# mLSTM layer in fp32: q, k, v and o projections as seven quarter products through DRAM, output projection beside the chunks

## The reference

```python
u = rmsnorm(h, mix_norm_g)
q, k, v, o_pre, if_pre = split(u @ w_in)       # 512, 512, 1024, 1024, 16 columns; k times 64 ** -0.5
# gates -> log_i, log_f; then over chunks, with a carried state (c_st, n_st, m_st):
scores = (qc @ kc.T) * exp(log_d - m_t)
num = w_inter * (qc @ c_st) + scores @ vc ;  den = w_inter * (qc @ n_st) + sum(scores)
hh = num / max(|den|, exp(-m_t)) ;  c_st, n_st updated from w_k and vc
h = h + (rms(hh) * norm_g * sigmoid(o_pre)) @ w_out
u = rmsnorm(h, ffn_norm_g)
h = h + (silu(u @ w_gate) * (u @ w_up)) @ w_down
```

## Time and profile before

| | us |
|---|---|
| median of 3 runs | 2203.44 (2202.58 to 2205.53) |
| the profiled execution | 2202.67 |
| its span, first to last instruction | 2200.7 |
| TensorE (PE) busy | 2170.1 |
| VectorE (DVE) busy | 1306.2 |
| ScalarE (ACT) busy | 883.4 |
| GpSimd (POOL) busy | 187.3 |

### The profile page before, as it was taken

The page is one execution under the profiler, slowest core; times in us unless marked ns, Lnnn a source line. Parts: engine busy times, 40 slices in busy tenths (PEclk is TensorE's granted clock), DMA queues, the critical chain, the costliest instruction groups (busy, mean ns, idle before and its releaser), DMA issues.

```text
span 2200.7 us, 29564 instructions
## 1 busy us (share of the span) xinstructions
PE 2170.1 (99%) x10600; PEld 1804.0 (82%) x10616; DVE 1306.2 (59%) x1990; ACT 883.4 (40%) x1520; POOL 187.3 (9%) x263
## 2 busy tenths in 40 slices
PE   7999999999999999999999999999999999999999
PEld 6888888878888888888888888888788888887887
DVE  6325666286656575678652366644865756656764
ACT  5224455253333333345422335552533333333443
POOL 2000110020101010100010011000210100101000
PEclk9999999999999999999999999999999999999999
DMA  4112124213232324863421221341333232367443
GB/s 145 57 57 56 51 68 152 97 67 120 96 115 100 114 99 142 286 227 115 154 77 38 68 58 49 113 164 48 91 101 115 93 107 93 103 200 239 149 127 112
DMA packets 215585, 245.80 MB, mean 112 GB/s; under 512 B 12096, under 2 KB 159552, under 8 KB 215488
## 3 DMA queue, kind: packets, MB, share of 16 engines
q1 hardware_dynamic: 194368, 171.60, 25.6%
q0 software_dynamic: 21120, 72.89, 8.7%
HBM read 187.31 MB, written 57.15 MB: 111 GB/s over the span
## 4 chain that ended last, share of the span: by engine, by line
PE 94%; DVE 3%; DMA 1%; ACT 1%; issue 1%; SPq 0%; POOL 0%; DVEq 0%; POOLq 0%; ACTq 0%
PE ps L1965 13%; PE ps L1968 13%; PE ps L1967 13%; PE ps L1644 8%; PE ps L1646 8%; PE ps L1645 8%; PE ps L2007 6%; PE ps L2011 6%; PE ps L2009 6%; PE ps L1631 2%; PE ps L1629 2%; PE ps L1630 2%; PE ps L1803 1%; DMA g_in<-ops_hbm 1%; PE ps L1799 1%; PE ps L1774 1%
## 5 line engine op out<-in xcount | busy, mean ns | idle before, releaser
L1409 DVE TENSOR_TENSOR ring<-raw_f,ring 128x512 fp32r<-128x512 f32 x308 | 212.4, 691 | 187.4 <-ACT ring L936 186.5
L1644 PE MATMUL ps<-u_lo,wp_hi 128*128 128x512 f32 x768 | 305.6, 398 | 1.5 <-DVE wp_lo L1093 1.2
L1646 PE MATMUL ps<-u_hi,wp_lo 128*128 128x512 f32 x768 | 300.1, 391 | 0.0
L1645 PE MATMUL ps<-u_hi,wp_hi 128*128 128x512 f32 x768 | 299.6, 390 | 0.0
L936 ACT CAST ring<-raw_f 128x512 fp32r<-128x512 f32 x308 | 191.2, 623 | 252.0 <-PE ps L1968 193.2
L1965 PE MATMUL ps<-u_lo,ring 128*128 128x512 f32 x704 | 274.7, 390 | 0.6 <-DVE t_op L1427 0.6
L1968 PE MATMUL ps<-u_hi,ring 128*128 128x512 f32 x704 | 274.0, 389 | 0.0
L1967 PE MATMUL ps<-u_hi,ring 128*128 128x512 f32 x704 | 273.9, 389 | 0.0
L2007 PE MATMUL ps<-ring,ring 128*128 128x512 f32 x616 | 240.9, 391 | 5.1 <-DVE ring L1532 5.1
L2011 PE MATMUL ps<-ring,ring 128*128 128x512 f32 x616 | 239.8, 389 | 0.0
L2009 PE MATMUL ps<-ring,ring 128*128 128x512 f32 x616 | 239.7, 389 | 0.0
(11 more groups left out here) (196 smaller groups left out, 3477.8 us busy)
## 6 DMA issues: line engine op xcount, KB each, us to landing
ops_hbm<-kept POOLq DMA_DIRECT2D x154, 256.0 KB, 2.4
g_in<-ops_hbm SPq DMA_DIRECT2D x154, 256.0 KB, 2.7
raw<-in_ml_w_in_dram SPq DMA_DIRECT2D x22, 1024.0 KB, 5.3
raw_f<-in_ffn_w_gate_dram SPq DMA_DIRECT2D x44, 512.0 KB, 4.7
raw_f<-in_ffn_w_up_dram SPq DMA_DIRECT2D x44, 512.0 KB, 4.6
b<-in_ffn_w_down_dram SPq DMA_DIRECT2D x88, 256.0 KB, 4.8
raw<-in_ml_w_in_dram SPq DMA_DIRECT2D x32, 512.0 KB, 3.8
x_in<-in_x_dram SPq DMA_DIRECT2D x16, 512.0 KB, 6.6
```

What stands on the lines that cost most here:

```text
L1409: nc.vector.tensor_tensor(four(ring[slot][:, 1, :]), feed_source(q, s), four(ring[slot][:, 0, :].bitcast(F32)), ALU.subtract).then_inc(w_l ...
L1644: pe.matmul(banks(bank), wh, u_lo[:, t, k, :], start=(k == 0), stop=False, skip_group_check=True)
L1645: pe.matmul(banks(bank), wh, u_hi[:, t, k, :], start=False, stop=False, skip_group_check=True)
L1646: last = pe.matmul(banks(bank), wl, u_hi[:, t, k, :], start=False, stop=(k == KD - 1), skip_group_check=True)
```

## The change

The first norm now makes the same operand as the second: four quarters of u and three sums, in 16 turn units (112 transposes) instead of 8 tiles (64 transposes). Four units of the second half stay beside the drain; twelve run after it. All q, k, v and o projections run ahead of the chunks as 12 groups of seven quarter products of 12 matmuls (84 units, 1008 matmuls a half). Their results go to DRAM (`proj_hbm`, 48 stores of 256 KB a half) and come back as three tiles of 512 KB a chunk (`qkc`, `vtc`, `og`). The sigmoid of o is taken before the store. The gates' product has 8 matmuls more, since the upper quarters of u now hold differences. The chunks have no projections beside them; they run the output projection of chunks c-1 and c-2, and DVE and ACT do the addition, the gating, the splitting and the second norm's rows there. The output weight is split with the head gain in it, in the first two chunks.

```diff
@@ TensorE, project, line 1778
+ def project(n):
+     g, q = unit_of(n)
+     kind = FEED[q]
+     bank = 2 * (g % 3) + (0 if kind in ON_X else 1)
+     pe.wait_ge(p_lo_done, h * PU + n + 1)
...
+ fresh = kind in ("P1", "P2", "P5")
+ w = pring[n % PRING]
+ for k in range(4):
+     now = slice(k * P, k * P + P)
+     pe.matmul(banks(bank), w[:, 0, now], moved(kind, 1, k), start=(fresh and k == 0), stop=False,
+               skip_group_check=True)
+     pe.matmul(banks(bank), w[:, 0, now], moved(kind, 0, k), start=False, stop=False,
+               skip_group_check=True)
+     last = pe.matmul(banks(bank), w[:, 1, now], moved(kind, 0, k), start=False, stop=(k == 3),
+                      skip_group_check=True)
+ last.then_inc(p_fed, 1)
@@ DVE, add_unit, line 1363
+ def add_unit(g, q):
+     k = pkept[g % 2]
+     x_bank, v_bank = 2 * (g % 3), 2 * (g % 3) + 1
+     kept_, bank, after = {1: (0, v_bank, 1), 4: (2, x_bank, 3), 5: (1, v_bank, 2)}[q]
+     dve.wait_ge(p_fed, h * PU + unit_at(g, q) + 1)
+     dve.wait_ge(p_act, act_at(h, g, after))
+     nc.vector.tensor_tensor(k[kept_][:, :], banks(bank), k[kept_][:, :], ALU.add).then_inc(p_dve, 1)
@@ ACT, the sigmoid of o, line 894
+     act.wait_ge(p_dve, dve_at(h, g, i + 1))
+     nc.scalar.activation(tile, tile, ACT.Exp, scale=-1.0).then_inc(o_step, 1)
+     act.wait_ge(o_step, step + 1)
+     nc.scalar.activation(tile, tile, ACT.Ln, bias=1.0).then_inc(o_step, 1)
+     act.wait_ge(o_step, step + 2)
+ else:
+     act.wait_ge(p_act, act_at(h, g, 4))
+     nc.scalar.activation(tile, tile, ACT.Ln, bias=1.0).then_inc(o_step, 1)
+     act.wait_ge(o_step, step + 1)
+ nc.scalar.activation(tile, tile, ACT.Exp, scale=-1.0).then_inc(o_gated, 1)
@@ SyncE, the loads of a chunk, line 492
+ def load_qkc(c):
+     if c >= 2:
+         sp.wait_ge(qw_done, h * 8 + c - 1)
+         sp.wait_ge(s_done, h * 8 + c - 1)
+         sp.wait_ge(k_turned, h * 8 + c - 1)
+     sp.dma_start(qkc[c % 2][:, :, :], proj_hbm[h, 0, c]).then_inc(qkc_loaded[c % 2], 16)
+ def load_vtc(c):
+     if c >= 1:
+         sp.wait_ge(v_turned, h * 8 + c)
+     sp.dma_start(vtc[:, :, :], proj_hbm[h, 1, c]).then_inc(vtc_loaded, 16)
+ def load_og(c):
+     if c >= 2:
+         sp.wait_ge(hglo_done, h * 8 + c - 1)
+     sp.dma_start(og[c % 2][:, :, :], proj_hbm[h, 2, c]).then_inc(og_loaded[c % 2], 16)
@@ TensorE, turn_unit, line 1726
+ def turn_unit(stage, n):
+     bank = unit_bank(stage, n)
+     at = stage * OP_UNITS
+     if n >= 6 or (stage == 0 and n >= 2):
+         pe.wait_ge(op_lo_done, at + n - 1)
+     elif n >= 4:
+         pe.wait_ge(op_lo_done, at + n - 2)
+     elif stage % 2 and n == 3:
+         pe.wait_ge(op_lo_done, at + 1)
+     elif stage == 2 and n >= 2:
+         pe.wait_ge(op_lo_done, at + n - 1)
@@ TensorE, ahead of the chunks and the chunks, line 1955
+ pe.wait_ge(colt_kept, h + 1)
+ pe.wait_ge(p_act, h * 4 * PG + 4 * PG)
+ pe.wait_ge(p_dve, h * 3 * PG + 3 * PG)
+ turn_v(0)
+ for c in range(TILES):
+     spread(c)
+     scores(c)
+     weights(c)
+     if c >= 2:
+         out_tile(c - 2, 1, 0, 4)
+     if c:
+         pe.wait_ge(dmat_done, h * 64 + c * 8 + 8)
+         turn_heads(c - 1)
+     if c >= 2:
+         out_tile(c - 2, 1, 4, KD)
+     state_sums(c)
+     outputs(c)
+     if c + 1 < TILES:
+         turn_v(c + 1)
+     if c:
+         out_tile(c - 1, 0, 0, KD)
+ out_tile(6, 1, 0, KD)
+ turn_heads(7)
+ pe.wait_ge(state_done, h * 32 + 32)
+ pe.wait_ge(num_kept, h * 16 + 16)
+ turn_unit(st + 1, 0)
+ turn_unit(st + 1, 1)
+ out_tile(7, 0, 0, KD)
+ pe.wait_ge(hg_done, h * 8 + 8)
+ turn_unit(st + 1, 2)
+ turn_unit(st + 1, 3)
+ out_tile(7, 1, 0, KD)
@@ ACT, split_out, line 934
+ def split_out(jj, k):
+     s = k // 4
+     if k % 4 == 0:
+         act.wait_ge(wo_loaded[s], h * 32 + 16 * (jj + 1))
+     nc.scalar.activation(wo[jj][0][:, k, :], wo_raw[s][:, k % 4, :], ACT.Copy,
+                          scale=head_g[:, k:k + 1]).then_inc(wohi_done, 1)
@@ DVE, the chunks, line 1510
+ for c in range(TILES):
+     weigh(c)
+     weigh_scores(c)
+     if c == 0:
+         for k in range(8):
+             split_out(0, k)
+     if c:
+         gate_heads(c - 1)
+     if c == 1:
+         for k in range(8):
+             split_out(1, k)
+     if c >= 2:
+         add_out(c - 2, 1)
+     if c:
+         hg_low(c - 1)
+     update_state(c)
+     head_scale_a(c)
+     head_scale_b(c)
+     if c >= 2:
+         norm2_rows(c - 2)
+     if c:
+         add_out(c - 1, 0)
@@ TensorE, the chunks and the output projection before, lines 1855 and 1926
- for c in range(TILES):
-     chunk(c, c == 0, c <= TILES // 2, c < TILES // 2)
...
- for i in range(TILES):
-     out_group(i, i, 0)
- pe.wait_ge(wolo_done, h * 4 + 4)
- for i in range(TILES):
-     out_group(i, i, 1)
-     for n in TURNS_AT[i]:
-         turn_unit(n)
```

1719 lines of the change are left out of this document (883 added, 836 removed).

## The result

The changed kernel takes 2271.97 us, median of 4 runs (2269.82 to 2274.07), against 2203.57 us before, median of 4 (2202.58 to 2205.53): a ratio of 1.031, 95% interval 1.029 to 1.033. The forecast was 2228 us with a range of 2204 to 2250. The direction was right; of 68 us that the change costs, 25 were foreseen.

What follows compares the result with a forecast made beforehand. The prediction took PE, busy in 99% of the span, to bound the kernel. Its terms, -13.2 + 19.9 + 22.0 - 3.5 = +25 us, on 2203.4 gave 2228 us, range 2204 to 2250.

Steps and rivals of the forecast that it cites:

- 76 us of new waiting: Whole kernel: PE's added waits, about 76 us, eat the 51 us of work taken from PE.
- The sum is 51.3 us less work: PE's work: 65.4 us gained on projections, 3.6 lost on the gates' product, 10.5 lost on transposes.
- rival B: First chunks: PE's clock falls to half pace in the gaps, some 8 us a half, 2244 us; 17%.
- No row before shows a gap long enough to try it: Earlier trace: no PE gap is long enough to test whether idling halves the clock; said of the half-pace rival, 17%.
- no wait above 1 us stands between them: Projections: sign that the forecast holds, PE's 2016 matmuls run at 0.227 us with no longer wait between them.
- The other loads ... I cost them at nothing: Tile loads from DRAM: issued early enough to hide behind projections and chunks, so 0 us.
- The last add and norm end at E+31: Tail: last add and norm end 31 us after E, the end of chunks 2 to 7; feed unit 4 starts at E+52.7.
- The check of 62 to 70 us: First start: sign that the forecast holds, the gates end at 62 to 70 us; forecast 66.4.
- About 0.2 us lie between an engine's end and the next one's start, as before L1277: Handover between engines: about 0.2 us each, used in following the chunks instruction by instruction.
- rival C: Full chunks: the chain through DVE and the wait for GpSimd's squares reach 22 us, 1.8 more a chunk, 2249 us; 10%.
- Chunks 2 to 7 at 20.24 us: Chunks 2 to 7: PE sets the pace at 20.24 us each, DVE stays behind PE's need.
- Rival A: Whole kernel: PE stays covered, new waits under 51 us; 2152 us with no new idle time; 15%.

Runs made afterwards that it cites:

- 0 of 16 at 0.95 us: The kernel before with 16 waits put into PE's drain units by chains of four small GpSimd writes, each 0.94 to 0.95 us; 2224.79 us, one run.
- the reordered one: Changed kernel with gates' parts, first chunks, residual transfers, tail sums and starts reordered: 2246.38 us, ratio 1.0180; with filling matmuls 2230.11 us, ratio 1.0132.
- the sixteen waits of 1.83 us: The kernel before with 16 waits put into PE's drain units by chains of eight small GpSimd writes; 2244.42 us, ratio 1.0181.
- waits of 3.6 us: The kernel before with 16 waits put into PE's drain units by chains of sixteen small GpSimd writes, each 3.62 us; 2289.6 us, one run.

## Why the prediction was wrong

**The waits: right in sum, and by luck in part.** 76 us of new waiting were counted, 79.9 measured. In the first chunks I had 15.8 a half (measured 10.2 and 12.2), before feed unit 4 12.4 (15.8 and 15.9), in the starts 19.9 + 22.0 less twice 7 of work, 28 more than before (24.2), and none in the projections (5.5 and 5.6). These four terms miss by -9, +7, -4 and +11 us, which nearly cancel. Slow work can also hide a wait: filling took some 20 us of slow pieces away in the changed kernel and only 12 us of time.

**PE's work: the step that failed.** "The sum is 51.3 us less work" priced every piece at the warm pace. 288 products less did bring 64.7 us (533.1 before, 468.4 now, from start to start, against 65.4 forecast), slow ones among them included. PE's busy time fell by 9.5 us and not by 51.3. What was lost is the pace behind the waits, 33.5 us in the trace, and the ends of the waits, some 8 us. I had this mechanism as rival B, with its price of half pace, and put it at 16 us, in the first chunks alone, at 17%; "after gaps of a microsecond in a warm stretch no row shows it" is still true, 0 of 16 at 0.95 us. But my own sum had longer waits in the starts and the tails too (3.2 us ahead of the projection of chunk 7, by its own times; measured 3.4, with 1.7 us of slow pieces behind it), and I asked for each only how long it was. The runs: filling the waits gives 12 us back in the changed kernel, and 11 in the reordered one, where the filling covers the starts too. So about a third of the 33.5 us is shown to be time that the clock alone costs. The rest the filling did not reach, or did not bring back, as in the first chunks, where something else ends the stage.

"No row before shows a gap long enough to try it" is wrong. The trace before has such a wait in a drain, 2.42 us long, and the products behind it keep the full pace:

```profile
2014.85 0.50 PE L2007 MATMUL ps<-ring,ring 128*128 128x512 f32 x1 [2.42 <-DVE ring L1532]
2015.19 0.40 PE L2009 MATMUL ps<-ring,ring 128*128 128x512 f32 x1
2015.43 0.40 PE L2011 MATMUL ps<-ring,ring 128*128 128x512 f32 x1
```

This row should have been in the argument, though alone it would have misled: of the sixteen waits of 1.83 us, ten look like it and six do not.

**"no wait above 1 us stands between them" (the projections): wrong**, 9.4 us. The step "80 units x 12 x 0.227 = 217.9" took as shown that the projections run as the feed does, since they are built like it, but beside the feed stand no gates. Moving the gates' parts alone showed it.

**"The other loads ... I cost them at nothing": wrong.** I had looked at when tiles are asked for, not at what stands in front of them: 4 MB for the residual and 2 MB of weight in a stage of 43 us. The bound that I gave for it (a load as slow as the weight's 9.7 us) was short of the 15.2 measured. The stage took only 2.5 and 3.1 us over the forecast; with the order alone changed it took 45.7 us in the first half, with the transfers alone 42.7, with both 37.2.

**The tails: +9.0 us each.** "The last add and norm end at E+31": the add ended at E+31.9, the norm at E+36.9, through ACT's sum of squares and a DVE operation of 0.16 us that took 1.51 beside GpSimd. GpSimd's 4.5 us in each tail were not in the sum at all, though the earlier trace rows come from this very place; I had added 2.5 only to the starts. The clock took 2.9; some 1.6 us of the 9.0 stay open.

**The starts: right within 4.4 and 2.7 us.** 66.4 forecast, 70.8 measured; 39.9 and 42.6. In the second, 2.6 us are slow pieces behind a wait of 4.3 us. In the first, the last low part ended at 63.5 us and not at 60.9 (58.4 and the 2.5 for GpSimd). Beside GpSimd two weights' low parts took 3.45 us together, not 1.4, but behind 44 us PE, ACT and DVE wait for one another in turn, as told above. Behind the last low part the gates' product ran at half pace for eight products, 1.6 us. The check of 62 to 70 us was just missed.

**A term without its row.** "About 0.2 us lie between an engine's end and the next one's start, as before L1277": the earlier trace rows do not show it. L1277 begins 0.13 us behind the start of GpSimd's squares and lies beside them. It is one more DVE operation stretched beside GpSimd (1.80 us), not a wait for the squares, as rival C reads it.

**Chunks 2 to 7 at 20.24 us: right**, 101.24 / 5 = 20.25; rival C falls. Rival A falls as well: the waits were 80 us, not under 51.

## What to carry to other kernels

A wait on an engine that is otherwise always busy costs more than its length. On these kernels a wait of PE cost its length and some 0.45 us at its ends; waits of 1.8 us were followed in 6 cases of 16, waits of 3.6 us in 13, by half pace that cost another 1.6 us or more; this change had traded 51 us of work for 80 us of waiting, and 42 of the 51 went with it. Price each new wait by its length, and look at the granted clock of a stretch before you call its work cheap. When a reordering shows nothing, look at who releases the wait now: in the first chunks a DVE chain and a transfer seem to have ended together, and only the run with both changes gained.
